# Key norms of an RWKV-7 recurrence: block-ones sums on all 128 rows in place of per-token sums and a spread product

## What is computed

```python
kk = (k * lp['rwkv_kk'].reshape(RWKV_HEADS, HEAD_DIM)).astype(jnp.float32)
kk = kk / jnp.maximum(jnp.sqrt(jnp.sum(kk * kk, -1, keepdims=True)), 1e-12)
k = k * (1 + (a - 1) * lp['rwkv_ka'].reshape(RWKV_HEADS, HEAD_DIM))
...
S = S * w_t[:, :, None, :] + sa[..., None] * (kk_t * a_t)[:, :, None, :] + v_t[..., None] * k_t[:, :, None, :]
```

## Time and profile before

| | |
|---|---|
| median of 3 runs | 2596.23 us (2593.48 to 2600.16) |
| time of the profiled execution | 2598.37 us |
| span of its profile | 2596.6 us |
| PE busy | 2394.8 us (92%) |
| PE weight load busy | 2092.8 us (81%) |
| DVE busy | 1207.4 us (46%) |
| ACT busy | 786.4 us (30%) |
| POOL busy | 520.0 us (20%) |

### The profile page before, as it was taken

The page is one execution under the profiler, slowest core; times in us unless marked ns, Lnnn a source line. Parts: engine busy times, 40 slices in busy tenths (PEclk is TensorE's granted clock), DMA queues, the critical chain, the costliest instruction groups (busy, mean ns, idle before and its releaser), DMA issues. The chain is left out here.

```text
span 2596.6 us, 47684 instructions
## 1 busy us (share of the span) xinstructions
PE 2394.8 (92%) x19959; PEld 2092.8 (81%) x19959; DVE 1207.4 (46%) x2324; ACT 786.4 (30%) x1437; POOL 520.0 (20%) x374
## 2 busy tenths in 40 slices
PE   5998998999857998988998999999999999989998
PEld 3777884454436888887886999977999999989998
DVE  4542225555524344555555544467333333346665
ACT  4332125565513333212224332222111111123332
POOL 4001210000121131000000443341323323323332
PEclk7997998999968999988897999999999999999999
DMA  7435422101253221111003111133111111131221
GB/s 284 145 122 161 131 65 110 34 1 49 79 163 137 76 93 65 66 51 51 7 3 131 49 45 41 53 124 102 44 49 50 41 49 49 41 91 46 79 79 46
DMA packets 160568, 201.60 MB, mean 78 GB/s; under 512 B 14905, under 2 KB 144250, under 8 KB 156834
## 3 DMA queue, kind: packets, MB, share of 16 engines
q1 hardware_dynamic: 154722, 182.81, 21.8%
q0 software_dynamic: 5632, 15.74, 2.1%
HBM read 170.68 MB, written 31.99 MB: 78 GB/s over the span
## 5 line engine op out<-in xcount | busy, mean ns | idle before, releaser
L165 POOL CAST w_hi<-w_raw 128x1024 fp32r<-128x1024 f32 (+1 forms) x115 | 124.9, 1086 | 1352.3 <-DMA w_raw<-in_w_in 477.3
L173 PE MATMUL pP_u<-h_hi,w_hi 128*128 128x352 f32 x1056 | 341.0, 323 | 0.3 <-PEq L2952 0.3
L174 PE MATMUL pP_u<-h_lo,w_hi 128*128 128x352 f32 x1056 | 338.5, 321 | 0.0
L175 PE MATMUL pP_u<-h_hi,w_lo 128*128 128x352 f32 x1056 | 338.2, 320 | 0.0
L167 POOL TENSOR_TENSOR w_lo<-w_raw,w_hi 128x1024 fp32r<-128x1024 f32 (+1 forms) x115 | 280.9, 2443 | 9.2
L173 PEld LDWEIGHTS pP_u<-h_hi,w_hi 128*128 128x128 f32 x1056 | 198.1, 188 | 0.7 <-issue 0.6
L174 PEld LDWEIGHTS pP_u<-h_lo,w_hi 128*128 128x128 f32 x1056 | 198.4, 188 | 0.0
L175 PEld LDWEIGHTS pP_u<-h_hi,w_lo 128*128 128x128 f32 x1056 | 197.9, 187 | 0.0
L3240 DVE TENSOR_TENSOR conv<-conv,conv_sig 128x1056 f32<-128x1056 f32 x22 | 50.2, 2283 | 312.4 <-ACT conv_sig L3208 312.4
L173 PE MATMUL pP_d<-a_piece_hi,w_hi 128*128 128x352 f32 x528 | 173.2, 328 | 10.5 <-DVE a_piece_lo L3398 8.4
L3407 DVE TENSOR_TENSOR a_piece_lo<-aT,a_piece_hi 128x1408 fp32r<-128x1408 f32 (+1 forms) x71 | 135.8, 1917 | 92.6 <-ACT a_piece_hi L3336 92.6
(11 more groups left out here) (514 smaller groups left out, 5168.9 us busy)
## 6 DMA issues: line engine op xcount, KB each, us to landing
w_raw<-in_w_up SPq DMA_DIRECT2D x44, 512.0 KB, 4.2
ybT<-in_w_ada SPq DMA_DIRECT2D x9, 2048.0 KB, 7.9
w_raw<-in_w_in SPq DMA_DIRECT2D x30, 512.0 KB, 4.3
kv_ring<-in_pool_kv SPq DMA_DIRECT2D x80, 128.0 KB, 2.3
w_raw<-in_w_down SPq DMA_DIRECT2D x20, 512.0 KB, 3.7
pair_scratch<-hT SPq DMA_DIRECT2D x3, 2752.0 KB, 9.8
cx<-in_pool_c POOLq DMA_DIRECT2D x64, 128.0 KB, 3.0
cx<-in_pool_c SPq DMA_DIRECT2D x64, 128.0 KB, 3.0
```

The lines of the kernel that those rows point to most:

```text
L165: engine.tensor_copy(hi, source).then_inc(done, 1)
L173: nc.tensor.matmul(out, w_hi, x_hi, start=start, stop=False)
L174: nc.tensor.matmul(out, w_hi, x_lo, start=False, stop=False)
L175: return nc.tensor.matmul(out, w_lo, x_hi, start=False, stop=stop)
```

## The change

The squares are multiplied by the full 128x128 `headsum`, with `across`, so that every partition gets the sum of its own head for every token. The root is taken on all 1056 columns of all 128 rows, back into `sq`, and DVE takes maximum and reciprocal of that whole table, the reciprocal in two pieces (704 and 352 columns) around the `mix` of the receptance. `kk` is then a product of SBUF operands only. `token_spread` goes from this stage, and so does the PSUM tensor `pN_e`. PE's product for a waits for `rooted` instead of `kk_out`. On ACT the Sigmoid of the decay comes ahead of the root, and Exp waits for `kk_out` too, since `E` lies on the slot of `sq`.

```diff
--- before.py
+++ after.py
@@ -1826,12 +1826,11 @@
         sem = ctx.enter_context(StageSemaphores(nc)).new
         pA = ctx.enter_context(nc.psum_tensor("pA_e", [128, 3, 512], F32))
         pB = ctx.enter_context(nc.psum_tensor("pB_e", [128, 3, 512], F32))
-        pN = ctx.enter_context(nc.psum_tensor("pN_e", [128, 512], F32))
         hi_ready, h_split, ready, xl_ready, head_mm, big_mm, head_old, tail_old, head_mix, tail_mix = (
             sem(f"rp_{n}") for n in ("hi_ready", "h_split", "ready", "xl", "head_mm", "big_mm", "head_old", "tail_old",
                                      "head_mix", "tail_mix"))
-        w_mm, w_out, a_mm, a_out, sq_out, norm_mm, rooted, inverse, spread_mm, kk_out, scanned, exps, widened, products = (
-            sem(f"rp_{n}") for n in ("w_mm", "w_out", "a_mm", "a_out", "sq", "norm_mm", "rooted", "inverse", "spread", "kk",
+        w_mm, w_out, a_mm, a_out, sq_out, norm_mm, rooted, inverse, kk_out, scanned, exps, widened, products = (
+            sem(f"rp_{n}") for n in ("w_mm", "w_out", "a_mm", "a_out", "sq", "norm_mm", "rooted", "inverse", "kk",
                                      "scanned", "exps", "widened", "products"))
         bonus_mm, bonus_ok, chain, first_high = (
             sem(f"rp_{n}") for n in ("bonus_mm", "bonus_ok", "chain", "first_high"))
@@ -1844,7 +1843,6 @@
         v = V[:, 64:64 + T]
         E = slots[7][:, 0:1040].rearrange("p (c t) -> p c t", t=65)
         ES = slots[7][:, 1040:1080].rearrange("p (b t) -> p b t", t=5)
-        norms = R["norms"][:, 0]
         half_life = float(np.exp(-0.5))
         out_of = lambda n: pA if n == 0 else pB
         pair_out = O["pair_scratch"]
@@ -1923,15 +1921,13 @@
                         pe.wait_ge(xl_ready, 1)
                     across(R["lora"][0:64, 128 * p:128 * p + 128], R["xl"][0:64]).then_inc(w_mm, 1)
                     big(n + 1, 0)
+                    pe.wait_ge(w_out, p + 1)
                     pe.wait_ge(sq_out, p + 1)
-                    token_sums(nc, S, pN, sq).then_inc(norm_mm, 1)
+                    across(S["headsum"], sq).then_inc(norm_mm, 1)
                     big(n + 1, 1)
                     big(n + 1, 2)
-                    pe.wait_ge(w_out, p + 1)
-                    pe.wait_ge(inverse, p + 1)
-                    token_spread(nc, S, pA, norms).then_inc(spread_mm, 1)
                     big(n + 2, 0)
-                    pe.wait_ge(kk_out, p + 1)
+                    pe.wait_ge(rooted, p + 1)
                     across(R["lora"][64:128, 128 * p:128 * p + 128], R["xl"][64:128]).then_inc(a_mm, 1)
                     big(n + 2, 1)
                     big(n + 2, 2)
@@ -1972,14 +1968,14 @@
                     act.wait_ge(head_mix, n + 1)
                     act.wait_ge(tail_mix, n + 1)
                     nc.scalar.activation(sq, k, ACT.Square, scale=col("kk")).then_inc(sq_out, 1)
-                    act.wait_ge(norm_mm, p + 1)
-                    nc.scalar.activation(norms[:, 0:16], pN[:, 0:16], ACT.Sqrt)
-                    nc.scalar.activation(norms[0:32, 16:18], pN[0:32, 16:18], ACT.Sqrt).then_inc(rooted, 1)
                     act.wait_ge(w_mm, p + 1)
                     nc.scalar.activation(thirds(lw), pA[:, :, 0:PIECE], ACT.Sigmoid, bias=col("w0")).then_inc(w_out, 1)
+                    act.wait_ge(norm_mm, p + 1)
+                    nc.scalar.activation(thirds(sq), pA[:, :, 0:PIECE], ACT.Sqrt).then_inc(rooted, 1)
                     head(n + 1)
                     tail(n + 1)
                     act.wait_ge(scanned, p + 1)
+                    act.wait_ge(kk_out, p + 1)
                     nc.scalar.activation(E[:, :, 1:65], cum[:, 0:SEQ].rearrange("p (c t) -> p c t", t=64), ACT.Exp, scale=-half_life)
                     nc.scalar.activation(ES[:, :, 1:5], cum[:, SEQ:T].rearrange("p (b t) -> p b t", t=4), ACT.Exp,
                                          scale=-half_life).then_inc(exps, 1)
@@ -2045,17 +2041,15 @@
                     if p:
                         bonus_of(p - 1)
                     mix(n, k)
-                    dve.wait_ge(rooted, p + 1)
-                    nc.vector.tensor_scalar(norms[:, 0:16], norms[:, 0:16], 1e-12, None, ALU.max)
-                    link(nc.vector.tensor_scalar(norms[0:32, 16:18], norms[0:32, 16:18], 1e-12, None, ALU.max))
-                    nc.vector.reciprocal(norms[:, 0:16], norms[:, 0:16])
-                    nc.vector.reciprocal(norms[0:32, 16:18], norms[0:32, 16:18]).then_inc(inverse, 1)
                     dve.wait_ge(w_out, p + 1)
                     nc.vector.tensor_tensor_scan(cum, R["scan"][:, 0:T], lw, 0.0, ALU.mult, ALU.add).then_inc(scanned, 1)
+                    dve.wait_ge(rooted, p + 1)
+                    link(nc.vector.tensor_scalar(sq, sq, 1e-12, None, ALU.max))
+                    nc.vector.reciprocal(thirds(sq)[:, 0:2], thirds(sq)[:, 0:2]).then_inc(inverse, 1)
                     mix(n + 1, r)
-                    dve.wait_ge(spread_mm, p + 1)
-                    flat = pA[:, :, :].rearrange("p i n -> p (i n)")[:, 0:T]
-                    nc.vector.scalar_tensor_tensor(kk, k, col("kk"), flat, ALU.mult, ALU.mult).then_inc(kk_out, 1)
+                    nc.vector.reciprocal(thirds(sq)[:, 2], thirds(sq)[:, 2]).then_inc(inverse, 1)
+                    dve.wait_ge(inverse, 2 * p + 2)
+                    nc.vector.scalar_tensor_tensor(kk, k, col("kk"), sq, ALU.mult, ALU.mult).then_inc(kk_out, 1)
                     dve.wait_ge(kk_out, p + 1)
                     nc.vector.memset(E[:, :, 0:1], 1.0)
                     link(nc.vector.memset(ES[:, :, 0:1], 1.0))
```

## The result

The changed kernel takes 2608.34 us (median of 5 runs, 2606.12 to 2609.83), the kernel before 2595.21 us in the runs beside it. The ratio is 1.0043 with a 95% interval of 1.0032 to 1.0053: **slower by 13.1 us**, where 10.3 had been forecast.

The account below looks back on a forecast made before the run. The prediction took the chain from a's product through Sigmoid, widening and DVE's products to the mix as the bound. Three pairs with 0.7 + 2.5 us and one with 0.7 gave 10.3 us longer, 2598.4 to 2608.7 (2606.5 at the median's level); range 2599.5 to 2613.

Parts of the forecast that it names:

- What bounds: At a pair's end: the chain of a's product, Sigmoid, widening, seven DVE products and mix; PE waited 9.7 us in total.
- DVE: Around the receptance's mix: reciprocals on 704 and 352 columns take 4.65 and 2.4 us, so `kk` comes 1.8 us later.
- it starts at 921.05 in place of 917.93, 3.1 us later: ACT's Exp of `E`, waiting for `kk_out`; less 2.4 us of idle time, `widened` comes 0.7 us later.
- The saved table load ... nothing: On ACT, the saved load of 1.28 us lies in time in which ACT waits anyway, so it gains nothing.
- POOL: At the end of three pairs, cast and subtraction hold DVE's products 3.3 us in place of 0.84, 2.5 us more.
- PE ends 2.2 us earlier: End of the value block: PE's earlier end makes POOL's cast ask at 929.6, inside DVE's run of products.
- The sum: Whole kernel: three pairs with 0.7 + 2.5 us and one with 0.7, 10.3 us longer.
- 1: Pair's end: POOL's subtraction doesn't get between DVE's products; 2.8 us longer, 2599; chance 0.27 together with the full-width rival.
- 2: DVE's reciprocal is much slower (10 ns a column) or locks POOL out; 15.5 us longer, 2612; chance 0.10.
- 3: PE is the bound after all, so each pair loses the spread's 2.2 us; 2587.6 us; chance 0.04.
- 4: Full-width norms delay nothing that is late; unchanged, 2596; chance 0.27 together with the rival on POOL's subtraction.
- A longer stop doesn't show a longer slow stretch: PE's clock after its waits: longer idle time costs 0, with 1 us a pair to both sides.

Follow-up runs that it names:

- e3: Changed kernel with 18 small products whose result nobody reads where the spread was, in each pair; 2614.0 us, ratio 1.0058 to the kernel before.
- e1: Changed kernel without ACT's wait for `scanned` in front of the Exp, so one wait is left; 2606.7 us, ratio 1.0039 to the kernel before.
- e9: Kernel before with one line more: ACT's Exp also waits for `kk_out`; 2608.9 us, ratio 1.0039 to the kernel before.
- e5: Changed kernel timed and traced a second time, with no edit; 2609.5 us, ratio 1.0052 to the kernel before.
- e2: Changed kernel with POOL's split at a pair's end held until the first half of the value's mix is done; 2603.9 us, ratio 1.0021.
- e4: Changed kernel with E and ES in a free part of hT, so Exp needn't wait for kk; 2585.3 us, ratio 0.9947 to the kernel before.
- e10: Changed kernel with E and ES in a free part of hT and POOL's split held for the value's mix; 2582.2 us, ratio 0.9938.

## Why the forecast was right, and where it was off

**What bounds.** Right: PE's wait for the first half of the value's mix, set by the chain of a's product, Sigmoid, widening and DVE's products. It grew from 9.7 to 29.0 us in all; none of the other waits of PE for an engine in the stage grew by more than 2.2 us.

**PE.** Right: the product on all rows replaced the sums at nearly the same price (1.94 us, before 2.00), the spread's 2.2 us went, no wait arose, and none of it reached the time (e3).

**DVE.** Right to a tenth: 4.55 and 2.35 us for the reciprocals (4.65 and 2.4 forecast, 6.25 ns a column); `kk` 1.6 us later (1.8 forecast). The forecast's estimate of 8.3 ns from the divide's repeat count of 8 (the Trainium skill, VectorE: DVE Perf Modes, walkthrough of the 8-slice pipeline) is not what the chip took: at the 0.96 GHz of that page the measured rate is 6 cycles a column. That its sum of 13 us lies near the 13.1 measured is chance: the term that it rests on, a second piece of 3.1 us, took 2.35.

**ACT.** Here the step "it starts at 921.05 in place of 917.93, 3.1 us later" was mis-sized: it put the new wait on the Exp alone. The Exp started 4.3 us later, counted from the pair's first matmul. With two waits in front of it, one stands on the table load that comes ahead, so its 1.28 us were no longer hidden. "The saved table load ... nothing" was right for that load and blind for the other. After the 2.42 us of idle time 1.85 us were left and not 0.7. e1 took the load from the chain and the run of products came 1.35 us earlier against `kk`.

**POOL.** Right in kind and place, too large in size: 2.79 us of holding in place of 3.3, since the cast came late in the second product and held DVE 0.65 us only. More than before: 1.95, forecast 2.5. The forecast's reason "PE ends 2.2 us earlier" was not needed: with PE's end put back the clash is the same (e3), and a run of DVE that is later by 0.2 us is enough for it (e9).

**The sum.** Three pairs with 1.85 + 1.95 = 3.8 us and one with 1.85 make 13.25, forecast 3 x 3.2 + 0.7 = 10.3. Two errors of opposite sign are in this: the chain was forecast 1.15 us too short in four pairs (4.6 us), the holding 0.55 us too long in three (1.6 us). That the forecast came within 3 us of the measured time is in part their cancelling. In the trace the four pairs are longer by 3.8, 3.8, 4.2 and 1.1 us, 12.9 in all; the last two differ from the sum by the clock, which stayed low for 4.2 us after the second wait where it was 3.4 before, and for 4.5 us after the third where it was 6.0.

**The rivals.** 1 (the subtraction doesn't get between) fell: 2.14 us on one product. 2 fell: the rate is that of the rows, and POOL's cast (910.17) and subtraction (911.29) ran beside the long reciprocal at 1.04 and 2.40 us, as in the rows where nothing holds them, so POOL isn't held by it. 3 and 4 fell with PE's wait.

**The clock.** "A longer stop doesn't show a longer slow stretch" held, nearly: after waits of 9.7 us PE worked at the 1.2 GHz level for 3.4 to 4.5 us in the first trace and for 4.9 to 5.0 us in e5, after the waits of 3.2 us of the kernel before for 3.4, 3.4 and 6.0 us. In the sum that is 12.1 and 14.8 us against 12.8.

## What to carry to other kernels

Follow a new wait to everything that is queued behind it on its engine, instructions that stand in no line of the source included: a table load that sits between the wait and its user is work too, and with two waits one of them may hang on it. A helper engine that shares a path with the bound one should be given its moment (e2), since a shift of 0.2 us can put two of its instructions into the chain (e9). A buffer shared by two uses is a dependence: here giving `E` its own place turned a change that cost 0.4% into a gain of 0.5%, and moving the read that frees PSUM ahead of other work made it 1.0%.

## What was unexpected in the hardware

- A reciprocal of 352 and of 704 columns takes 2.353 and 4.553 us, 6.25 ns a column, and a cast and a subtraction of POOL run beside it undisturbed (1.04 and 2.40 us), where beside two-input products they took up to 2.10 (e4) and 3.23 us.
- The order between POOL and DVE is decided by hundredths: with the cast 0.02 us after the start of the second large BK product (e4) DVE was held 0.84 us, with the cast 0.07 us ahead of it (e9) 2.96 us.
- Whether the granted clock falls after a wait of about 3 us isn't certain: it did in three of three cases in the kernel before, for 3.4 to 6 us, and in e10, after 2.5 us, at the first two waits but not at the third.
